# Half of the projection matmuls read their moving operand and write their PSUM bank in descending order of columns

## The chip, the cores and the metric

The kernel runs on one core of one Trainium2 chip. The metric is the device time of one execution in microseconds (us). TensorE (PE in the profile) does the matmuls, VectorE (DVE), ScalarE (ACT) and GpSimd (POOL) the elementwise work, and SyncE (SP) issues most DMAs. The time before is 3540.6 us, the median of two runs.

## The reference, cut to what matters

A sequence of 512 tokens with 1024 features goes through five blocks. Four of them have a mixer (differential attention, HGRN2, sliding-window attention, differential attention again), an output projection, a feed-forward part and a gated addition; the fifth has retention, a linear recurrence and a convolved feed-forward part. Nearly all the arithmetic is dense products of the activations with weight matrices:

```python
for i in range(DEPTH):
    ...
    h = layer_norm(ALPHA * h + y, ln_g[i, 0], ln_b[i, 0])
    u = jnp.square(jax.nn.relu(h @ w_up[i])) @ w_down[i]
    h = layer_norm(ALPHA * h + u, ln_g[i, 1], ln_b[i, 1])
    h = h + jax.nn.sigmoid(h @ w_ple_gate[i]) * (p[i] @ w_ple[i])
```

with `w_up` 1024 x 4096 and `w_down` 4096 x 1024. Each product is wanted at about float32 precision.

## The kernel before, in words

**Tiling.** Activations lie in SBUF features first: a tile such as `xh` is [128, 8, 512], that is 8 blocks of 128 features by all 512 tokens. Weights come from HBM as a stream of slabs of 1024 input features by 256 output features (1 MB each), into a ring of three or four slots. A slab used for one product is a unit of PE's work.

**Three passes.** Every operand is split into a high part and a low part of type float32r: `whi` and `wlo` of the weights, `xh` and `xl` or `gh` and `gl` of the activations. A product is the sum of three matmuls: high by high, high by low, low by high. POOL makes `whi` from `raw` (line 468), DVE makes `wlo` (line 1768).

**The loops of a unit.** A unit with features as output rows is eight calls of `feature_chunk`, one for each block k of 128 input features. A call loops over the two blocks j of 128 output features. For each it calls `passes`, whose three matmuls (lines 498, 499, 500) hold 128x128 weights in the array, stream all 512 tokens as the moving operand, and add into one whole PSUM bank, `proj[:, 2 * (u % 2) + j, :]`. So a unit fills two banks, and the next unit uses the other two of `proj`. ACT and DVE read both banks when the unit is done, always in ascending order, and release them.

**The other two forms.** `half_chunk` (lines 619 to 621) does the same for half of the tokens, 256 columns at a time, around the normalisations, where the second half of the tokens isn't ready yet. `token_chunk` (lines 531 to 533) makes values with tokens as output rows: the activations of token block `st` are the stationary operand, and 256 columns of `whi` or `wlo` the moving one; its four token blocks fill the halves of two banks.

**What stays apart.** The mixers' own matmuls (scores, transposes, values) write the `mix` banks and have their own lines: line 816 works on slices of heads in HGRN2 with a strided moving operand, line 1042 makes values of retention in plain float32. The first unit of the kernel is written out by hand in `first_chunks` (line 677), with another order: each pass goes over k and j, so that the bank changes at every matmul.

**What sets the order.** Every engine's instructions stand in a fixed order, written out by hand. PE waits at the start of a unit for the slab's split (`split_done`) and for the release of the banks used two units before (`PLAN.released`). PE's order is the program's.

Of the kernel before, what the change touches and what calls it, by code (L numbers as in the profile page):

```python
# [144 lines left out]
def cols(hf):  # L145
    return slice(0, S) if hf is None else slice(hf * HALF, (hf + 1) * HALF)
# [65 lines left out]
def build(nc, stream, xin, pin, pos, vecs, relb, onehot, eye, picks, decay, out):  # L212
    with ExitStack() as ctx:
# [203 lines left out]
        @block.sync  # L417
        def _(sp):

            for t in range(4):  # L420
                sp.dma_start(raw[0][:, 2 * t:2 * t + 2].rearrange("p k n -> p (k n)"), stream[0, :, 512 * t:512 * t + 512]).then_inc(first_in[t], 16)
            for n in range(1, N_SLABS):
                if n < 3:
                    sp.wait_ge(x_in[n + 1], 16)
                elif n == 3:
                    sp.wait_ge(raw_in[2], 16)
                else:
                    sp.wait_ge(unit_done, PLAN.last_unit[BEFORE[n]] + 1)
                if n == RETURNED:
                    sp.wait_ge(gl_ready, 4 * (G_GEN["mixed"] + 1))  # L430
                if n == 2:
                    for dst, src in (vec[:, :], vecs), (ident[:, :], eye), (tab[:, :], onehot), (rb[0:32, :], relb):
                        sp.dma_start(dst, src).then_inc(loaded, 16)
                sp.dma_start(raw[SLOT[n]][:, :, :].rearrange("p k n -> p (k n)"), stream[n]).then_inc(raw_in[SLOT[n]], 16)

            for hf in range(2):
                for t in range(KT // 2):
                    p2 = slice(2 * t, 2 * t + 2)
                    sp.wait_ge(M("final_out"), KT // 2 * hf + t + 1)
                    sp.dma_start(out[:, p2, cols(hf)], fin[:, p2, cols(hf)]).then_inc(M("stored"), 16)  # L440
            sp.wait_ge(M("stored"), KT * 16)
# [50 lines left out]

        @block.tensor
        def _(pe):
            def passes(out, wparts, xparts, first, last, check=False):

                (wh, wl), (ah, al) = wparts, xparts
                nc.tensor.matmul(out, wh, ah, start=first, stop=False, skip_group_check=check)  # L498
                nc.tensor.matmul(out, wh, al, start=False, stop=False, skip_group_check=check)  # L499
                return nc.tensor.matmul(out, wl, ah, start=False, stop=last, skip_group_check=check)  # L500
# [9 lines left out]
            def feature_chunk(u, k, kn, w0, operand):  # L510

                slot = SLOT[PLAN.unit_slab[u]]
                oh, ol = operand
                for j in range(2):
                    c = slice(j * P, (j + 1) * P)
                    last = passes(proj[:, 2 * (u % 2) + j, :], (whi[slot][:, w0 + k, c], wlo[slot][:, w0 + k, c]),
                                  (oh[:, k, :], ol[:, k, :]), k == 0, k == kn - 1)
                return last

            def token_chunk(u, k, kn, operand, c0=0, width=256, banks=(0, 1)):  # L520


                slot = SLOT[PLAN.unit_slab[u]]
                oh, ol = operand
                per = 4 // len(banks)
                for st in range(4):
                    o = proj[:, 2 * (u % 2) + banks[st // per], (st % per) * width:(st % per + 1) * width]
                    t = slice(st * P, (st + 1) * P)
                    w = slice(c0, c0 + width)
                    ah, al, wh, wl = oh[:, k, t], ol[:, k, t], whi[slot][:, k, w], wlo[slot][:, k, w]  # L530
                    nc.tensor.matmul(o, ah, wh, start=k == 0 and st % per == 0, stop=False, skip_group_check=True)  # L531
                    nc.tensor.matmul(o, ah, wl, start=False, stop=False, skip_group_check=True)  # L532
                    last = nc.tensor.matmul(o, al, wh, start=False, stop=k == kn - 1, skip_group_check=True)  # L533
                return last
# [10 lines left out]
            def whole_unit(u, which, gen=None, token=False, kn=8, w0=0, operand=None):  # L545
                begin_unit(u)
                op = operand or (X if which == "x" else G)
                for k in range(kn):
                    if gen is not None:
                        operand_wait(which, gen, k)  # L550
                    last = token_chunk(u, k, kn, op) if token else feature_chunk(u, k, kn, w0, op)
                last.then_inc(unit_done, 1)
# [10 lines left out]
            def out_chunks(layer, first, end):  # L563

                for i in range(first, end):
                    j, k = DA_TAIL[i] if layer % 3 == 0 else TAIL[i]
                    u = PLAN.at[f"out{layer}"][1] + j
                    if k == 0:
                        begin_unit(u)
                    out_operand(layer, k)  # L570
                    last = feature_chunk(u, k, 8, 0, X)
                    if k == 7:
                        last.then_inc(unit_done, 1)

            def out_halves(layer, first, end):

                for j, k in HALVES[first:end]:
                    u = PLAN.at[f"out{layer}"][1] + j
                    if k == 0:
                        pe.wait_ge(split_done, PLAN.unit_slab[u] + 1)  # L580
                    out_operand(layer, k)
                    last = half_chunk(u, k, 0, X, True, mix[:, j - 2, :])
                    if k == 7:
                        last.then_inc(M("half_done"), 1)
# [24 lines left out]
            def half_chunk(u, k, hf, operand, own_banks, bank=None):  # L609

                slot = SLOT[PLAN.unit_slab[u]]
                oh, ol = operand
                for j in range(2):
                    c = slice(j * P, (j + 1) * P)
                    o = proj[:, 2 * (u % 2) + hf, cols(j)] if own_banks else proj[:, 2 * (u % 2) + j, cols(hf)]
                    if bank is not None:
                        o = bank[:, cols(j)]
                    wh, wl, ah, al = whi[slot][:, k, c], wlo[slot][:, k, c], oh[:, k, cols(hf)], ol[:, k, cols(hf)]
                    nc.tensor.matmul(o, wh, ah, start=k == 0 and (j if own_banks else hf) == 0, stop=False, skip_group_check=True)  # L619
                    nc.tensor.matmul(o, wh, al, start=False, stop=False, skip_group_check=True)  # L620
                    last = nc.tensor.matmul(o, wl, ah, start=False, stop=k == 7, skip_group_check=True)  # L621
                return last
# [59 lines left out]
            def da_mixer(d, layer):  # L682
# [3 lines left out]
                def chunk(g, c):  # L686
                    u = u0 + 3 * g + c // 8
                    k = c % 8
                    if k == 0 and u > 1:
                        begin_unit(u)  # L690
                    if g == 0 and c < 8:
                        operand_wait("g", gen, k)
                    if layer == 0 and g == 0 and c < 16 and k % 2 == 0:
                        pe.wait_ge(*((first_lo, k // 2 + 4) if k < 6 else (split_done, 2)))
                    last = token_chunk(u, k, 8, G) if c // 8 == 2 else feature_chunk(u, k, 8, 0, G)
                    if k == 7:
                        last.then_inc(unit_done, 1)
# [82 lines left out]
            def hg_mixer(layer):  # L780
# [3 lines left out]
                def chunk(g, c):  # L784
                    u = u0 + 4 * g + c // 8
                    k = c % 8
                    if k == 0:
                        begin_unit(u)
                    if g == 0 and c < 8:
                        operand_wait("g", gen, k)  # L790
                    last = token_chunk(u, k, 8, G) if c // 8 == 2 else feature_chunk(u, k, 8, 0, G)
                    if k == 7:
                        last.then_inc(unit_done, 1)
# [285 lines left out]
            for n in range(4):  # L1079
                whole_unit(u0 + 3 * n, "g")  # L1080
                for t in range(2):
# [3 lines left out]
                    for k in range(2):  # L1085
                        last = feature_chunk(u, k, 2, 4 * (n % 2) + 2 * t, (xh[:, 2 * n:2 * n + 2, :], xl[:, 2 * n:2 * n + 2, :]))
# [1606 lines left out]
```

## Time and profile before

| | |
|---|---|
| median of 2 runs | 3540.6 us (3539.72 to 3541.49) |
| the profiled execution's own time | 3541.19 us |
| its span (first to last instruction) | 3539.4 us |
| PE | 3501.5 us busy, 99% of the span |
| DVE, ACT, POOL | 1769.1, 960.5 and 633.1 us busy (50%, 27%, 18%) |
| DMA | 332.88 MB, mean 94 GB/s |

A matmul's row in the trace has a start and a duration. Consecutive matmuls overlap in the array, so their durations add up to more than the span; what a matmul costs in a dense stream is the distance from its start to the next start. The granted clock is the share of its full speed at which TensorE was let run.

### The profile page before, as it was taken

The numbers are of one execution on the slowest core, as the hardware profiler recorded it, in microseconds if no ns is written. First come the engines' busy times: TensorE is split into PE (matmuls) and PEld (weight loads), VectorE is DVE, ScalarE is ACT, GpSimd is POOL, SyncE is SP. The second block draws the span as 40 slices with busy tenths as digits, with TensorE's granted clock in tenths as the row PEclk, the third lists the DMA queues.
The fourth block names the chain that finished last, engine by engine and source line by source line (L and its number), as shares of the span: only waits on it lengthen the run. The fifth ranks groups of instructions, "written<-read, shape, count | busy, mean of one in ns | idle before, by whom it ended". The sixth has DMA issues, their size and how long they took to land.

```text
span 3539.4 us, 44299 instructions
## 1 busy us (share of the span) xinstructions
PE 3501.5 (99%) x18416; PEld 2956.1 (84%) x18416; DVE 1769.1 (50%) x2276; ACT 960.5 (27%) x1679; POOL 633.1 (18%) x372
## 2 busy tenths in 40 slices
PE   9999999999999999999999999999999999999999
PEld 7788888889888888688888878888888888898887
DVE  5454334556653346763336455553474346563434
ACT  3562001334220013630113356210141215120102
POOL 2112111200031112031112111311121111211110
PEclk9999999999999999999999999999999999999999
DMA  5322222222122223122222221222222122322222
GB/s 206 108 74 94 95 95 94 103 85 85 65 103 98 95 84 111 60 90 95 95 97 94 101 84 72 98 96 95 84 80 99 72 95 95 107 96 95 96 95 72
DMA packets 65463, 332.88 MB, mean 94 GB/s; under 512 B 9795, under 2 KB 20291, under 8 KB 28532
## 3 DMA queue, kind: packets, MB, share of 16 engines
q1 hardware_dynamic: 44316, 303.50, 24.0%
q10 hardware_dynamic: 20952, 26.56, 2.3%
q8 instruction: 149, 2.44, 0.3%
q14 instruction: 46, 0.38, 0.0%
HBM read 326.22 MB, written 10.90 MB: 95 GB/s over the span
## 4 chain that ended last, share of the span: by engine, by line
PE 88%; DVE 6%; ACT 4%; issue 1%; POOL 1%; DMA 0%; DVEq 0%; ACTq 0%; POOLq 0%
PE proj L498 23%; PE proj L500 23%; PE proj L499 23%; PE proj L619 2%; PE proj L620 2%; PE proj L621 2%; PE proj L531 2%; PE proj L532 2%; PE proj L533 2%; DVE wlo L1768 1%; PE mix L709 1%; DVE s L1878 1%; ACT xh L1183 1%; ACT h L1186 1%; PE mix L735 1%
## 5 line engine op out<-in xcount | busy, mean ns | idle before, releaser
L468 POOL TENSOR_SCALAR whi<-raw 128x2048 fp32r<-128x2048 f32 x272 | 529.4, 1946 | 2676.3 <-DVE wlo L1768 1710.6
L498 PE MATMUL proj<-gh,whi 128*128 128x512 f32 x1952 | 775.3, 397 | 2.1 <-DVE wlo L1768 2.1
L500 PE MATMUL proj<-gh,wlo 128*128 128x512 f32 x1952 | 761.4, 390 | 0.0
L499 PE MATMUL proj<-gl,whi 128*128 128x512 f32 x1952 | 760.8, 390 | 0.0
L1768 DVE TENSOR_TENSOR wlo<-raw,whi 128x2048 fp32r<-128x2048 f32 x285 | 651.2, 2285 | 137.4 <-POOL whi L468 94.4
L498 PE MATMUL proj<-xh,whi 128*128 128x512 f32 x1760 | 692.8, 394 | 8.7 <-DVE wlo L1768 3.0
L500 PE MATMUL proj<-xh,wlo 128*128 128x512 f32 x1760 | 685.7, 390 | 0.0
L499 PE MATMUL proj<-xl,whi 128*128 128x512 f32 x1760 | 685.5, 389 | 0.0
L498 PEld LDWEIGHTS proj<-gh,whi 128*128 128x128 f32 x1952 | 367.0, 188 | 93.3 <-issue 15.6
L500 PEld LDWEIGHTS proj<-gh,wlo 128*128 128x128 f32 x1952 | 366.8, 188 | 77.5
L499 PEld LDWEIGHTS proj<-gl,whi 128*128 128x128 f32 x1952 | 367.1, 188 | 75.6 <-issue 1.9
L498 PEld LDWEIGHTS proj<-xh,whi 128*128 128x128 f32 x1760 | 330.8, 188 | 89.6 <-issue 11.5
L500 PEld LDWEIGHTS proj<-xh,wlo 128*128 128x128 f32 x1760 | 330.7, 188 | 69.6
L499 PEld LDWEIGHTS proj<-xl,whi 128*128 128x128 f32 x1760 | 331.0, 188 | 68.2 <-issue 1.4
L1487 ACT ACTIVATE rl<-proj 128x1024 f32<-128x1024 f32 x64 | 65.9, 1029 | 947.8 <-PE proj L500 929.2
L1861 DVE TENSOR_TENSOR h<-h,proj 128x1024 f32<-128x1024 f32 (+1 forms) x76 | 80.0, 1052 | 348.4 <-PE proj L500 325.3
L2302 DVE SCALAR_TENSOR_TENSOR hid<-proj,rl 128x1024 f32<-128x1024 f32 x64 | 78.4, 1224 | 317.7 <-ACT rl L1487 317.1
L619 PE MATMUL proj<-xh,whi 128*128 128x256 f32 x608 | 174.8, 288 | 3.5 <-POOL xl L463 2.2
L620 PE MATMUL proj<-xl,whi 128*128 128x256 f32 x608 | 171.9, 283 | 0.0
L621 PE MATMUL proj<-xh,wlo 128*128 128x256 f32 x608 | 171.8, 283 | 0.0
L531 PE MATMUL proj<-whi,gh 128*128 128x256 f32 x512 | 149.5, 292 | 0.0
L533 PE MATMUL proj<-whi,gl 128*128 128x256 f32 x512 | 144.8, 283 | 0.0
(321 smaller groups left out, 4333.0 us busy)
## 6 DMA issues: line engine op xcount, KB each, us to landing
raw<-in_stream SPq DMA_DIRECT2D x286, 1024.0 KB, 4.8
da_b<-bias_da ACTq DMA_DIRECT2D x16, 512.0 KB, 3.4
bias_da<-bias_rows ACTq DMA_DIRECT2D x8, 512.0 KB, 8.7
h<-in_x ACTq DMA_DIRECT2D x4, 512.0 KB, 8.7
bias_sw<-bias_table ACTq DMA_DIRECT2D x1, 2048.0 KB, 9.9
pf<-in_p ACTq DMA_DIRECT2D x4, 512.0 KB, 6.8
sw_b<-bias_sw ACTq DMA_DIRECT2D x4, 512.0 KB, 4.4
out_features<-fin SPq DMA_DIRECT2D x8, 256.0 KB, 2.4
```

The source lines that it names most:

```text
L468: nc.gpsimd.tensor_scalar(whi[SLOT[n]][:, :, :], raw[SLOT[n]][:, :, :], 1.0, 0.0, ALU.mult, ALU.add).then_inc(hi_done, 1)
L498: nc.tensor.matmul(out, wh, ah, start=first, stop=False, skip_group_check=check)
L499: nc.tensor.matmul(out, wh, al, start=False, stop=False, skip_group_check=check)
L500: return nc.tensor.matmul(out, wl, ah, start=False, stop=last, skip_group_check=check)
L531: nc.tensor.matmul(o, ah, wh, start=k == 0 and st % per == 0, stop=False, skip_group_check=True)
L533: last = nc.tensor.matmul(o, al, wh, start=False, stop=k == kn - 1, skip_group_check=True)
L619: nc.tensor.matmul(o, wh, ah, start=k == 0 and (j if own_banks else hf) == 0, stop=False, skip_group_check=True)
L620: nc.tensor.matmul(o, wh, al, start=False, stop=False, skip_group_check=True)
L621: last = nc.tensor.matmul(o, wl, ah, start=False, stop=k == 7, skip_group_check=True)
L1768: V.tensor_tensor(wlo[SLOT[n]][:, :, :], raw[SLOT[n]][:, :, :], whi[SLOT[n]][:, :, :].bitcast(F32), ALU.subtract).then_inc(*own.sig(split_ ...
L1861: ins = V.tensor_tensor(o, o, y, ALU.add)
L2302: V.scalar_tensor_tensor(hid[:, :, :], banks(u), 0.0, rl[:, :, :], ALU.max, ALU.mult).then_inc(*own.sig(rel["dve"]))
```

## The change

Three edits, all in the block of PE. In `passes`, a new argument `down` reverses the output, and both moving operands, along their columns; `feature_chunk` sets it for j = 1. In `token_chunk` the odd token blocks get their output and their moving weights reversed. In `half_chunk` j = 1 does. Since output and moving operand are both reversed, each column of the result still lands in its old place. The stationary operands, the order of the instructions, the flags that start and end an accumulation and all waits stay as they are, and `first_chunks` and the matmuls of the mixers are not touched. All three matmuls of one pass group, in all eight k, go in the same direction for a given bank (or, in `token_chunk`, half bank), so a bank is accumulated in one direction throughout.

```diff
-            def passes(out, wparts, xparts, first, last, check=False):
+            def passes(out, wparts, xparts, first, last, check=False, down=False):
                 (wh, wl), (ah, al) = wparts, xparts
+                if down:
+                    out, ah, al = out[:, ::-1], ah[:, ::-1], al[:, ::-1]
                 nc.tensor.matmul(out, wh, ah, start=first, stop=False, skip_group_check=check)
...
             def feature_chunk(u, k, kn, w0, operand):
...
-                                  (oh[:, k, :], ol[:, k, :]), k == 0, k == kn - 1)
+                                  (oh[:, k, :], ol[:, k, :]), k == 0, k == kn - 1, down=j == 1)
...
             def token_chunk(u, k, kn, operand, c0=0, width=256, banks=(0, 1)):
...
                     ah, al, wh, wl = oh[:, k, t], ol[:, k, t], whi[slot][:, k, w], wlo[slot][:, k, w]
+                    if st % 2:
+                        o, wh, wl = o[:, ::-1], wh[:, ::-1], wl[:, ::-1]
...
             def half_chunk(u, k, hf, operand, own_banks, bank=None):
...
                     wh, wl, ah, al = whi[slot][:, k, c], wlo[slot][:, k, c], oh[:, k, cols(hf)], ol[:, k, cols(hf)]
+                    if j:
+                        o, ah, al = o[:, ::-1], ah[:, ::-1], al[:, ::-1]
```

## Rows read from the trace of the kernel before

**Rows 1.** The page: span, then busy time of each engine.
```profile
span 3539.4 us, 44299 instructions
...
PE 3501.5 (99%) x18416; PEld 2956.1 (84%) x18416; DVE 1769.1 (50%) x2276; ACT 960.5 (27%) x1679; POOL 633.1 (18%) x372
```

**Rows 2.** The page: the chain that ended last, share of the span by engine.
```profile
PE 88%; DVE 6%; ACT 4%; issue 1%; POOL 1%; DMA 0%; DVEq 0%; ACTq 0%; POOLq 0%
```

**Rows 3.** Waits of PE, its longest three: us in total, times, longest.
```profile
PE mix L595 <- DVE s L1878: 5.1, 5, 2.2
PE proj L498 <- DVE wlo L1768: 5.1, 7, 1.5
PE mix L735 <- DVE post_on L2012: 3.9, 6, 0.8
```

**Rows 4.** The view of the cores: span and mean granted TensorE clock.
```profile
core 0: 3539.4 us, clock 0.998
```

**Rows 5.** A stretch: PE, PEld, DVE, ACT, POOL busy (x instructions), PEclk, DMA share, GB/s.
```profile
1200.00:1300.00 100.00, 100.00 (x442) 82.81 (x442) 39.24 (x25) 11.27 (x11) 17.28 (x9) 1.00 0.28 98
```

**Rows 6.** PE's groups by line, whole span: count, busy us, mean ns.
```profile
L498 PE MATMUL proj<-gh,whi 128*128 128x512 f32 x1952 | 775.3, 397 | 2.1 <-DVE wlo L1768 2.1
...
L498 PE MATMUL proj<-xh,whi 128*128 128x512 f32 x1760 | 692.8, 394 | 8.7 <-DVE wlo L1768 3.0 <-DVE xl L2168 2.5 <-POOL xl L463 1.5
...
L619 PE MATMUL proj<-xh,whi 128*128 128x256 f32 x608 | 174.8, 288 | 3.5 <-POOL xl L463 2.2 <-issue 1.3
...
L531 PE MATMUL proj<-whi,gh 128*128 128x256 f32 x512 | 149.5, 292 | 0.0
...
L619 PE MATMUL proj<-gh,whi 128*128 128x256 f32 x448 | 127.9, 286 | 0.0
...
L498 PE MATMUL proj<-ph,whi 128*128 128x512 f32 x64 | 25.7, 402 | 0.0
...
L619 PE MATMUL mix<-xh,whi 128*128 128x256 f32 x32 | 9.6, 302 | 0.0
```

**Rows 7.** Timeline of PE, a feed-forward unit: start us, duration us, one feature chunk.
```profile
660.26 0.39 PE L498 MATMUL proj<-xh,whi 128*128 128x512 f32 x1
660.49 0.39 PE L499 MATMUL proj<-xl,whi 128*128 128x512 f32 x1
660.72 0.39 PE L500 MATMUL proj<-xh,wlo 128*128 128x512 f32 x1
660.94 0.39 PE L498 MATMUL proj<-xh,whi 128*128 128x512 f32 x1
...
662.98 0.39 PE L498 MATMUL proj<-xh,whi 128*128 128x512 f32 x1
```

**Rows 8.** Timeline of PE, a token chunk and what follows it.
```profile
90.00 0.28 PE L533 MATMUL proj<-whi,gl 128*128 128x256 f32 x1
...
92.63 0.40 PE L498 MATMUL proj<-gh,whi 128*128 128x512 f32 x1
```

**Rows 9.** Timeline of PE in the hand-written first unit, four matmuls a row.
```profile
14.10 1.07 PE L677 MATMUL proj<-gh,whi 128*128 128x512 f32 x4
15.01 1.07 PE L677 MATMUL proj<-gl,whi 128*128 128x512 f32 x4
15.92 1.07 PE L677 MATMUL proj<-gh,wlo 128*128 128x512 f32 x4
```

**Rows 10.** Timeline of PE at line 816, moving step 2, then runs of 4.
```profile
732.76 1.07 PE L816 MATMUL mix<-hg_q,hg_m 128*128 128x128 f32 x8
733.59 0.48 PE L498 MATMUL proj<-gh,whi 128*128 128x512 f32 x1
...
742.83 1.05 PE L816 MATMUL mix<-hg_q,hg_m 128*128 128x128 f32 x8
743.64 0.48 PE L498 MATMUL proj<-gh,whi 128*128 128x512 f32 x1
```

**Rows 11.** Timeline of PE at line 1042: plain float32, two rows for each matmul.
```profile
2691.34 1.89 PE L1042 MATMUL mix<-rt_v,rt_s 128*128 128x256 f32 x8
2693.07 0.59 PE L1030 MATMUL mix<-rt_q,rt_k 128*128 128x256 f32 x2
```

## The prediction

> **What bounds the kernel now.** I read the page first: PE is busy for 3501.5 of 3539.4 us [rows 1], and the chain that ended last runs on PE for 88% of the span [rows 2]. The list of waits says the same from the other side: the longest three sources of idle time of PE are 5.1, 5.1 and 3.9 us in total [rows 3], and span less busy time leaves 38 us for all of them. The granted clock is 0.998 of full speed, which is the 2.4 GHz level [rows 4]. So the end is set by how fast matmuls follow each other, and a change to the stream of matmuls shows in full.
>
> A busy PE is not PE at its peak, so the next question is what one matmul costs. In a stretch of 100 us that holds nothing but matmuls of 512 columns there are 442 [rows 5], 0.226 us each. The timeline gives the same: twelve of them from 660.26 to 662.98, that is 2.72 / 12 = 0.227 us [rows 7]. For 256 columns, 22 follow each other from 90.00 to 92.63, or 0.120 us each [rows 8]. From the two, 256 more columns take 0.227 - 0.120 = 0.107 us, which is 2.4 columns in a ns, one a clock at the level granted. What is left of each matmul is a fixed part of 0.120 - 0.107 = 0.013 us, whatever its length. These two numbers, 0.107 us for 256 columns and 0.013 us for each matmul, are all that a reversed stream can change.
>
> **The change part by part.** Nothing is added or taken away, and no instruction changes its place on any engine; no wait is added. What changes is the step of two access patterns, from 1 to -1, in part of the matmuls.
>
> How many: the groups of line 498 hold 1952 + 1760 + 64 = 3776 matmuls [rows 6]; lines 499 and 500 have as many each, so 11328 in all, half of them with j = 1: 5664 of 512 columns. Line 619 has 608 + 448 + 32 = 1088 and line 531 has 512 [rows 6], each with two sister lines: (1088 + 512) x 3 = 4800, half of them reversed: 2400 of 256 columns. Together 8064 reversed matmuls. Each ns that a reversed matmul loses or wins is 8.1 us of the span, and 2% of the time, 71 us, is 8.8 ns for each.
>
> First cost, reading the moving operand backwards from SBUF. No row shows a descending read. The nearest are those of line 816: the moving operand has step 2 in the stretch from 732.76 to 733.59 (0.83 us for 8 rows) and runs of 4 in that from 742.83 to 743.64 (0.81 us) [rows 10]. Step 2 costs 0.02 us over 8 rows there, 2.5 ns each. They are plain float32, though, where a matmul takes several times as long: at line 1042, eight rows make four matmuls of 256 columns in 2693.07 - 2691.34 = 1.73 us, 0.43 us each [rows 11] against 0.120. So these reads had about four times the time for each column, and a read twice as slow would have hidden there. Bounds: nothing from below, and 2.5 ns x 8064 = 20 us as the price that a row shows. I take nothing, since a descending run of single steps touches the same words as an ascending one, and no more of them than a step of 2 does.
>
> Second cost, writing the bank backwards. Here no row is near: every write of the trace ascends in runs of 64 columns or more. The bound from below is nothing. The bound from above is the slowest stream that the trace has at this clock, the float32 rate [rows 11]: 0.43 - 0.12 = 0.31 us more for 256 columns and 0.62 for 512, so 5664 x 0.62 + 2400 x 0.31 = 4256 us, a time of about 7800 us. I take nothing, because the fixed part and the rate don't depend on where in PSUM the next write goes: in the hand-written first unit the bank changes at every matmul, and four matmuls take 15.92 - 15.01 = 0.91 us [rows 9], 0.2275 each, the same as where three in a row go to one bank [rows 7]. That is weak evidence: it shows that a jump between matmuls costs nothing, not that descending within one does.
>
> Third, the turn. The direction changes between the banks of a chunk and again at the next chunk: 2 turns in each of 11328 / 6 = 1888 feature chunks and 3264 / 6 = 544 half chunks, 4 in each of 1536 / 12 = 128 token chunks, 5376 in all. A turn could at best remove the fixed part: 5376 x 0.013 = 70 us. I take nothing: the rows of one chunk show the same 0.227 us from matmul to matmul whether the bank stays or changes [rows 7, 9], so the fixed part isn't the price of going back to column 0 of a bank.
>
> Fourth, what lies around. Consumers read the banks after the unit's last matmul as before. DVE, ACT and POOL are busy for at most half of the span [rows 1], their work isn't touched, and the slabs come in at the pace at which PE frees them.
>
> The sum against the profiled execution: 3539.4 + 0 us, with 1.8 us around the span in its own time of 3541.19 us, which is 0.6 us over the median. **Forecast: 3541 us.**
>
> **A rule against the change.** Every PSUM write seen ascends, and the 512-column rows run at one column a clock [rows 7]. The Trainium skill ("PSUM — Partial Sum Buffer", Specifications) states that PSUM has cachelines of 8 bytes, two float32 values, and that "any non-contiguous AP slows matmuls significantly"; "Advanced Engine Details and Errata" (PSUM Cachelines) wants every two consecutive elements contiguous. A step of -1 is adjacent but descending, and the rule doesn't say which it counts as. No row here tests it. If it counts as non-contiguous, the result is the first rival below.
>
> **The rivals.**
>
> (a) *Each reversed matmul streams at half rate.* The mechanism: at one column a clock, columns are taken two at a time, and a descending pair isn't taken as a pair, so that each column needs a turn of its own, on the reading or on the writing side. It speaks for it that 0.107 us for 256 columns leaves no slack at all, while everything strided in the trace runs at the slower float32 rate [rows 10, 11]. Against it: two neighbours in descending order still lie side by side. The price: 0.107 us for each 256 columns, 5664 x 0.214 + 2400 x 0.107 = 1212 + 257 = 1469 us, so 3541 + 1469 = 5010 us; some of PE's 38 us of waits would vanish, which gives about 5000. The side changes at 8.8 ns for each reversed matmul, some 8% of the loss for 256 columns: any real pairing fault lands far beyond.
>
> (b) *A small fixed price,* such as restarting a prefetch backwards: from 9 to 40 ns each, 3610 to 3860 us. The upper end is three times today's fixed part. Nothing in the trace speaks for it but that the fixed part exists.
>
> (c) *The turn helps,* as worked out above: 3541 - 70 = 3471 us, 2.0% faster, if each turn removes the whole fixed part. The equal distances of [rows 9] speak against it.
>
> (d) *The pattern is turned back,* so that the chip streams upwards anyhow: 3541 us, the same as the forecast.
>
> **How the numbers follow.** Forecast and (d), within 2% with a small price of up to 2.5 ns or a small gain: 0.57. (a) 0.29, with the float32 rate beyond it 0.02. (b) 0.08. (c) 0.04, half of it beyond 2%, and other gains no more. The likeliest case has a range of its own, 3525 to 3570 us: a fifth of the gain of (c) on one side, the 20 us of the step of 2 on the other. It holds 0.57 alone, so the range must take in (a): 3525 to 5015 us, which leaves out the float32 bound and most of (c). Faster by over 2%: 0.03, within 2%: 0.58, slower by over 2%: 0.39. Two per cent is about what a measurement of this kernel can tell from no change.
>
> **What would show it.** If I am right, the changed kernel has about 442 matmuls in a stretch of 100 us of a feed-forward part, and starts 0.227 us apart for both directions. If (a) is right, the timeline shows three starts 0.227 apart and then three about 0.44 apart, with some 300 matmuls in 100 us, DVE's and POOL's share falls to some 35 and 13% of a span of 5000 us, and PE's waits for DVE all but vanish. If (b), the second three are 0.24 to 0.27 apart. If (c), the first matmul after each turn starts 0.214 after the one before. The prediction fails at the second cost if descending writes are slow, and at the first if descending reads are; a kernel that reverses only one of the two would tell which.

## The result, and the profile after

The changed kernel takes 3603.95 us, the median of two runs (3602.96 to 3604.94), against 3540.6 us: a ratio of 1.0179, 95% interval 1.0135 to 1.0223. It is slower, by 63 us. That is just under the 2% that the text before used as its line; with two runs the interval reaches across that line. It is 7.9 ns for each of the 8064 reversed matmuls on average, but it isn't spread that way, as the rows show.

The page of the changed kernel, span, busy times and chain:

```profile
span 3601.2 us, 44299 instructions
...
PE 3566.6 (99%) x18416; PEld 2958.6 (82%) x18416; DVE 1763.9 (49%) x2276; ACT 959.6 (27%) x1679; POOL 630.7 (18%) x372
...
PE 88%; DVE 6%; ACT 4%; issue 1%; POOL 1%; DVEq 0%; ACTq 0%; POOLq 0%
```

The span is 61.8 us longer, PE's busy time 65.1 us, the other engines' busy times are within 5.2 us of those before [rows 1], and the chain has the same shares [rows 2]. So the loss is in PE's stream and nowhere else. Its waits and the clock say so too (waits of the changed kernel, the three that answer to [rows 3], and its view of the cores):

```profile
PE mix L599 <- DVE s L1884: 5.3, 5, 2.2
PE mix L741 <- DVE post_on L2018: 3.6, 6, 0.7
PE proj L500 <- DVE wlo L1774: 3.4, 7, 1.4
```
```profile
core 0: 3601.2 us, clock 0.999
```

The stretch of [rows 5] again, and one feature chunk of the changed kernel on the timeline, from its first matmul to that of the next. Lines 498 to 500 have become 500 to 502; the first three rows ascend, the next three descend:

```profile
1200.00:1300.00 100.00, 100.00 (x431) 80.70 (x430) 36.14 (x23) 10.41 (x10) 17.15 (x9) 1.00 0.27 95
```
```profile
670.07 0.40 PE L500 MATMUL proj<-xh,whi 128*128 128x512 f32 x1
670.31 0.39 PE L501 MATMUL proj<-xl,whi 128*128 128x512 f32 x1
670.54 0.39 PE L502 MATMUL proj<-xh,wlo 128*128 128x512 f32 x1
670.77 0.40 PE L500 MATMUL proj<-xh,whi 128*128 128x512 f32 x1
671.00 0.40 PE L501 MATMUL proj<-xl,whi 128*128 128x512 f32 x1
671.24 0.40 PE L502 MATMUL proj<-xh,wlo 128*128 128x512 f32 x1
671.47 0.40 PE L500 MATMUL proj<-xh,whi 128*128 128x512 f32 x1
```

431 matmuls in 100 us instead of 442, and 1.40 us for six instead of 1.36 [rows 7]. The reader should see that the first ascending matmul, which the change doesn't touch, is followed after 0.24 us, not 0.227. The ten ns steps of the timeline are too coarse for more, so I collected the starts in ns: in each of 887 stretches of two feature chunks (twelve matmuls in a row), the distance from start to next start, and of these the median at each place. The same for 257 stretches of half chunks. A half chunk is one call of `half_chunk`, with 256 columns. Here are all kernels of this study; "up" and "down" are the directions of the first three and the last three matmuls of a chunk:

```
distance in ns after matmul          1   2   3   4   5   6   sum | 256 columns, mean of twelve
before          (up / up)           227 227 227 227 227 227  1362 | 120.0
the change      (up / down)         238 232 227 234 239 231  1401 | 118.8
read_only       (up / down)         238 232 227 234 238 231  1400 | 118.8
write_only      (up / down)         227 227 227 227 227 227  1362 | 120.0
all_down        (down / down)       233 233 233 233 233 233  1398 | 118.3
by_k, even k    (up / up)           238 232 227 227 227 227  1378 |
by_k, odd k     (down / down)       232 240 231 233 233 233  1402 | 118.6
every_turn      (up down up / down up down) 238 231 228 234 232 231  1394 | 120.0 (not turned)
quads_down      (down / down)       233 233 233 233 233 233  1398 | 118.3
blocks32_down   (down / down)       232 231 232 231 232 231  1389 | 119.2
halves_swapped  (up / up)           227 227 227 227 227 227  1362 | 120.0
one_column_up   (up / up)           226 234 233 226 234 233  1386 | 113.7
one_column_down (down / down)       233 233 233 233 233 233  1398 | 118.0
small_down      (up / up, 256 down) 227 227 227 227 227 227  1362 | 118.3
pad256          (up / up)           227 227 227 227 227 227  1362 | 120.0
```

At 256 columns the mean hides a pattern: before, every distance is 120 ns; in the change the medians run from 115 to 122, and when all descend from 116 to 122.

A chunk of the change is 1401 - 1362 = 39 ns longer, and 1888 chunks x 0.039 = 74 us, more than the 62 us of the span. Where the difference lies shows when the distances of the two traces are subtracted matmul by matmul, since both have the same 18416 in the same order. The 9354 matmuls of 512 columns in long stretches (over 36 in a row) take 58.8 us more, 6.3 ns each. The other 1974, in short stretches between the mixers' matmuls, take 5.5 us more, only 2.8 ns each. The 4800 of 256 columns take 2.5 us less, and all the rest together is 0.2 us. So what a median from a dense stretch promises isn't met in full elsewhere.

### The profile page after: what moved, and what is told of

Same layout as the page of the kernel before. It is cut to its first block, busy times and chain, and to the rows that moved or that the text cites. A ratio compares the mean times of both kernels' runs of the same rounds, so it can differ in the third digit from the quotient of the medians.

```text
span 3601.2 us, 44299 instructions
## 1 busy us (share of the span) xinstructions
PE 3566.6 (99%) x18416; PEld 2958.6 (82%) x18416; DVE 1763.9 (49%) x2276; ACT 959.6 (27%) x1679; POOL 630.7 (18%) x372
## 4 chain that ended last, share of the span: by engine, by line
PE 88%; DVE 6%; ACT 4%; issue 1%; POOL 1%; DVEq 0%; ACTq 0%; POOLq 0%
PE proj L500 23%; PE proj L501 23%; PE proj L502 23%; PE proj L625 2%; PE proj L627 2%; PE proj L626 2%; PE proj L535 2%; PE proj L536 2%; PE proj L537 2%; DVE wlo L1774 1%; PE mix L715 1%; DVE s L1884 1%; ACT xh L1189 1%; ACT h L1192 1%; PE mix L741 1%
## 5 line engine op out<-in xcount | busy, mean ns | idle before, releaser
L500 PE MATMUL proj<-gh,whi 128*128 128x512 f32 x1952 | 791.7, 406 | 1.7 <-DVE wlo L1774 1.7
L501 PE MATMUL proj<-gl,whi 128*128 128x512 f32 x1952 | 774.7, 397 | 0.0
L500 PE MATMUL proj<-xh,whi 128*128 128x512 f32 x1760 | 707.8, 402 | 6.3 <-DVE xl L2174 2.5
L501 PE MATMUL proj<-xl,whi 128*128 128x512 f32 x1760 | 698.6, 397 | 0.0
```

## The experiments

The times in this section are medians, each with its ratio to runs of the kernel before taken on the same chip (3540.1 to 3540.9 us).

### All downwards

```diff
-  ..., k == 0, k == kn - 1, down=j == 1)
+  ..., k == 0, k == kn - 1, down=True)
-                    if st % 2:
+                    if True:
-                    if j:
+                    if True:
```

> Every matmul of the three forms, of both output blocks and all token blocks, descends, so that direction no longer changes within or between chunks (only against the mixers' own matmuls). Turn theory: the 63 us of the change are the price of 5376 turns, 11.8 ns each; with no turns left the time is 3541 us (within 10). Descending theory: each of the 8064 descending matmuls costs 7.9 ns, and with twice as many the time is 3541 + 127 = 3668 us. Start-to-start distance of 512 columns: 0.227 us by the turn theory, 0.235 by the other.

3602.37 us, ratio 1.0175 (1.0157 to 1.0193). Neither theory gives this: without turns the time doesn't come back, and with twice as many descending matmuls it doesn't double. The table shows 233 ns at every place: a steady descending stream of 512 columns costs 6 ns each, and 11328 x 0.006 = 68 us, less 4800 x 0.0017 = 8 us at 256 columns, gives 60 us against the 61 measured (subtracted matmul by matmul: 67.2 us more at 512 columns, 4.5 less at 256). In the change the same loss has another make-up: three descending matmuls cost 18 ns over 227, and the remaining 21 ns of the 39 come with the mixture of directions, partly on ascending matmuls (11 and 5 ns).

### Direction by input block

```diff
-  ..., k == 0, k == kn - 1, down=j == 1)
+  ..., k == 0, k == kn - 1, down=k % 2 == 1)
-                    if st % 2:
+                    if k % 2:
-                    if j:
+                    if k % 2:
```

> Direction goes with the block k of input features (odd k descends), not with the output block j: as many descending matmuls as in the change, but one turn in each feature or half chunk instead of two, and one instead of four in a token chunk: 2560 turns instead of 5376. Turn theory: 3541 + 2560 x 0.0118 = 3571 us. Descending theory: 3604 us, as the change. By the turn theory the slow distances stand behind the turn only, in the first three matmuls of each new direction, and the last three of the six are back at 0.227 us.

3587.25 us, ratio 1.0133 (1.0117 to 1.0149), between the two. As many descending matmuls as in the change cost less when they come six at a time. The table shows both parts: after a turn upwards 238 and 232 ns and then 227 four times, so here the ascending stream recovers after two matmuls (11 + 5 = 16 ns for the turn); the descending six take 1402 ns, four more than six steady ones. The sum for two chunks, 16 + 36 + 4 = 56 ns, x 944 pairs = 53 us, and the 256-column matmuls take 2.9 us less by the traces: 50 us, against 46 measured. On the timeline of this kernel, the third to the sixth matmul of an ascending chunk, with 0.22 and 0.23 us between the starts:

```profile
672.96 0.39 PE L502 MATMUL proj<-xh,wlo 128*128 128x512 f32 x1
673.18 0.39 PE L500 MATMUL proj<-xh,whi 128*128 128x512 f32 x1
673.41 0.39 PE L501 MATMUL proj<-xl,whi 128*128 128x512 f32 x1
673.63 0.39 PE L502 MATMUL proj<-xh,wlo 128*128 128x512 f32 x1
```

### Only the read, and only the write

```diff
-                    out, ah, al = out[:, ::-1], ah[:, ::-1], al[:, ::-1]
+                    ah, al = ah[:, ::-1], al[:, ::-1]       # read_only; write_only: out = out[:, ::-1]
```

and likewise in the token and half chunks.

> Only the moving operand is reversed where the change reverses it; the banks are written upwards, so the columns of those blocks come out in mirrored order (the values are not the reference's). If the price lies on the reading side: 3604 us and the same distances as in the change (0.238, 0.232, 0.227, 0.234, 0.239, 0.231 for the six matmuls of a feature chunk). If it lies on the writing side: 3541 us and 0.227 throughout.

> Only the output is reversed where the change reverses it; the moving operand is read upwards, so the columns of those blocks come out in mirrored order (the values are not the reference's). If the price lies on the writing side: 3604 us and the distances of the change. If it lies on the reading side: 3541 us and 0.227 us throughout. If both sides share it, each of the two runs shows a part of the 63 us.

The read alone: 3604.48 us, ratio 1.0181 (1.0165 to 1.0197), with the distances of the change to within 1 ns. The write alone: 3540.75 us, ratio 1.0000 (0.9990 to 1.0010), 227 and 120 ns throughout. The same stretch of both, read first:

```profile
1200.00:1300.00 100.00, 100.00 (x430) 80.74 (x429) 36.94 (x23) 9.64 (x11) 17.19 (x9) 1.00 0.26 91
```
```profile
1200.00:1300.00 100.00, 100.00 (x443) 82.84 (x442) 40.09 (x25) 10.48 (x10) 17.20 (x9) 1.00 0.28 102
```

So the whole loss is on the reading side, and writing a bank from its last column to its first costs nothing. The interval of the run with only the read reversed, with four runs, stays under 2%.

### Small matmuls alone

```diff
-  ..., k == 0, k == kn - 1, down=j == 1)
+  ..., k == 0, k == kn - 1, down=False)
-                    if st % 2:
+                    if True:
-                    if j:
+                    if True:
```

> All 4800 matmuls of 256 columns (half and token chunks) descend, all 11328 of 512 ascend as before. The run in which everything descended had 0.1183 us from start to start at 256 columns against 0.120 ascending, and 0.233 against 0.227 at 512. If the gain at 256 columns is a property of the descending read: 3540.9 - 4800 x 0.0017 = 3533 us, 0.2% faster, and 0.227 at 512 columns throughout. If it only came about beside descending 512-column matmuls: 3541 us.

3536.49 us, ratio 0.9988 (0.9980 to 0.9997): faster by about 4 us, half of what was expected. The distances came out as expected, 118.3 and 227 ns, and the page shows 6.3 us less of PE's busy time:

```profile
PE 3495.2 (99%) x18416; PEld 2949.3 (83%) x18416; DVE 1768.7 (50%) x2276; ACT 960.2 (27%) x1679; POOL 631.3 (18%) x372
```

The span is 4.7 us shorter (3534.7 against 3539.4), so 1.6 us went into idle time; many of these matmuls stand around the normalisations. One such wait is that for DVE's sums, 5.9 us now against 5.1 [rows 3]:

```profile
PE mix L599 <- DVE s L1884: 5.9, 5, 2.2
```

Subtracted matmul by matmul, the 4800 take 5.0 us less, not the 8 that the medians promise. The gain at 256 columns doesn't depend on descending 512-column neighbours. It is small, 0.1%, but it is a version that beats both kernels.

Something else changes at 256 columns: the record of the weight load. One of its rows before, and the same in this run:

```profile
L620 PEld LDWEIGHTS proj<-xl,whi 128*128 128x128 f32 x608 | 116.5, 192 | 0.1
L626 PEld LDWEIGHTS proj<-xl,whi 128*128 128x128 f32 x608 | 114.5, 188 | 0.1
```

The median load has 192 ns in every run whose 256-column matmuls all read upwards (in swapped halves too), and 188 or 189 in those in which they all descend, in groups or column by column, or in which the load reads one column. Beside 512 columns the load has 188 ns both in the kernel before and when all descend, and it ends 36 ns before the next matmul starts, or 41. So a longer load isn't what makes the steady 233 ns. That the gain at 256 columns comes from the shorter load would fit, but isn't shown.

### Groups of four columns, and of 32

```diff
-                if down:
-                    out, ah, al = out[:, ::-1], ah[:, ::-1], al[:, ::-1]
+                blk = lambda a: a.rearrange("p (n c) -> p n c", c=4)[:, ::-1, :]      # and c=32
+                out, ah, al = blk(out), blk(ah), blk(al)
```

in all three forms, for every matmul.

> All matmuls of the three forms take their columns in groups of four (16 bytes), the groups from last to first, each group upwards, in the read and the write. Order-within-a-group theory (the descending read loses because neighbours come in the wrong order inside a group that is fetched at once): 3541 us, 0.227 and 0.120 us. Group-order theory (it loses because the groups are fetched from last to first): as when everything descends, 3602 us, 0.233 and 0.118 us. If a jump after every four columns is costly in itself, reading or writing: over 3700 us.

> As the run with groups of four, with groups of 32 columns (128 bytes): each group upwards, the groups from last to first, 15 backward jumps in 512 columns. If the price comes from fetching ahead in larger pieces than 128 bytes, or from the overall direction: 0.233 us and 3602 us again. If pieces of up to 128 bytes are fetched as one and only steps down between neighbouring pieces of 16 bytes cost: near 0.227 us and 3545 us.

Groups of four: 3601.86 us, ratio 1.0175 (1.0161 to 1.0189), with the distances of the run in which everything descends. The order inside 16 bytes plays no part, and a backward step after every four columns costs no more than a plain descent. Groups of 32: 3593.33 us, ratio 1.0150 (1.0135 to 1.0165), 231.5 ns: still 4.5 of the 6 ns, although a descending step comes only every 32 columns. These runs reverse the groups in the write as well; that the loss is again on the reading side is taken over from the run with the write alone, not tested here.

### The halves swapped

```diff
+                blk = lambda a: a.rearrange("p (n c) -> p n c", c=a.shape[-1] // 2)[:, ::-1, :]
```

> Every matmul of the three forms takes the second half of its columns first, then the first half, each half upwards: one backward jump inside the stream. Direction theory (the price belongs to a stream that moves downwards from group to group): 3541 us, 0.227 and 0.120 us, or at most the price of one jump. Phase theory (all that counts is at which address the stream starts against the weight load): the distances change as when everything descends, 0.233 us at 512 columns.

3541.10 us, ratio 1.0002 (0.9993 to 1.0012), 227 and 120 ns. One backward jump of 512 columns' span is free, and the stream may start in its middle. It is not a price per jump either: 15 jumps cost 4.5 ns, 0.3 each, while one costs under 0.1 ns when the two traces are subtracted matmul by matmul, and 127 jumps or 511 steps cost 6 ns. Somewhere between two pieces of 256 columns and 16 of 32 the loss sets in; piece size and number of jumps change together here.

### A turn at every matmul

The edit is made in the kernel before; `feature_chunk` passes `down=j == 1`, and the 256-column forms stay upwards.

```diff
+                turned = lambda a, odd: a[:, ::-1] if odd else a
+                b = int(down)
-                nc.tensor.matmul(out, wh, ah, ...)
-                nc.tensor.matmul(out, wh, al, ...)
-                return nc.tensor.matmul(out, wl, ah, ...)
+                nc.tensor.matmul(turned(out, b), wh, turned(ah, b), ...)
+                nc.tensor.matmul(turned(out, 1 - b), wh, turned(al, 1 - b), ...)
+                return nc.tensor.matmul(turned(out, b), wl, turned(ah, b), ...)
```

> Feature chunks only: the middle one of three matmuls goes the other way, so the direction changes at each of the 11328 matmuls of 512 columns (bank and operand both reversed, values unchanged); 256-column matmuls ascend. Priced from the earlier runs: a descending matmul 6 ns, a turn to ascending 16 ns, a turn to descending 4 ns, 26 ns for each pair, 5664 x 0.026 = 147 us: 3688 us. If turns cost nothing when bank and operand are met again at the same end: 5664 x 0.006 = 34 us, 3575 us.

3594.51 us, ratio 1.0151 (1.0136 to 1.0166). My price list from the earlier runs was wrong: six turns in a chunk cost 32 ns with the three descending matmuls, less than two turns do in the change (39). Turns have no fixed price, and the table shows why adding prices fails: a disturbed matmul stands at 231 to 234 ns most of the time, whatever disturbed it, and 238 to 240 appear only at the first matmul after a turn upwards and the second after a turn downwards. Nor does every turn upwards cost 11 and 5 ns: at the third matmul of this run it leaves 228 ns and at the fifth 232, against 238 at the first. In the change and in the run by input block all turns upwards fall on the first matmul of a chunk, so those two runs can't tell the turn from its place.

### One stationary column

```diff
+                one = lambda a: a[:, 0:1].broadcast_to([P, P])
+                wh, wl = one(wh), one(wl)
```

> Everything ascends, but every stationary operand is one column read 128 times (step 0), so that the weight loads no longer sweep through SBUF; the values are not the reference's. If the sweep of the weight load is what the moving read meets (meeting theory), the distances of 512 and 256 columns change from 0.227 and 0.120 us: if its fixed part of 0.013 us is the price of meetings, to 0.216 and under 0.110, a time near 3400 us. If the weight load's place doesn't matter: 0.227, 0.120 and 3541 us.

> As the run with one stationary column, but every moving operand and output descends (values not the reference's). Meeting theory (a descending read loses because it meets the weight load's sweep differently): the same distances as the ascending run with one column. Stream theory (the descending read is slower by itself): 0.006 us more at 512 columns than the ascending run with one column, 0.002 less at 256, and some 60 us more in all.

Upwards: 3565.85 us, ratio 1.0070 (1.0055 to 1.0086). Downwards: 3599.76 us, ratio 1.0168 (1.0154 to 1.0182). Both theories miss. What the weight load reads does matter to an ascending stream: the distances become 226, 234 and 233 ns at 512 columns, and 114 instead of 120 at 256. (The values in the array change with it; that they set the time is unlikely, since the descending stream has the same values and keeps its 233 ns.) But the loads' sweep isn't the cause of the 13 ns that each matmul has beyond its columns: at 512 columns the fastest pass wins 1 ns of them, though at 256 columns 6 ns go, and the descending stream hardly notices the loads: 233 and 118 with one column as with 128. The groups of the ascending run with one stationary column show it too: a mean duration of 393 ns for the first pass, which is 394 in the kernel before [rows 6], and of 396 for the other two:

```profile
L501 PE MATMUL proj<-xl,whi 128*128 128x512 f32 x1760 | 697.0, 396 | 0.0
L502 PE MATMUL proj<-xh,wlo 128*128 128x512 f32 x1760 | 696.5, 396 | 0.0
L500 PE MATMUL proj<-xh,whi 128*128 128x512 f32 x1760 | 691.7, 393 | 8.0 <-DVE xl L2174 2.5 <-DVE wlo L1774 2.1 <-POOL xl L463 1.5
```

### The tiles moved

```diff
+        top[0] += 256
         hg_m = place("hg_m", [P, 2, S], at=top[0] + 6 * S * 4)
```

> The kernel before with the activation tiles xh, xl, gh, gl (and the small tiles behind them) moved up by 256 bytes in SBUF, so that each stream starts at another address against the weight load; order and directions as before. Address theory (0.227 us is what one relation of the two addresses gives; with one stationary column the ascending distances were 0.226, 0.234 and 0.233 us): the distances change by some ns, 3541 plus or minus 20 to 60 us. Direction theory: 0.227, 0.120 and 3541 us.

3540.12 us, ratio 1.0000 (0.9990 to 1.0009), 227 and 120 ns. Moving the activations by 256 bytes against the weights changes nothing, so a shift of that size between the two start addresses isn't what makes the 227 ns. Other shifts weren't tried.

## Why the prediction was right or wrong

**The frame held.** PE's stream sets the end; no other engine's busy time moved by more than 5.2 us, and the loss of 62 us of span is 65 us of PE's busy time. The count of 8064 reversed matmuls held. The sign for being right did not: 431 matmuls in the stretch instead of 442. The time of 3604 us lies in the range of 3525 to 5015 us, and the median is within 2%. But that is luck: the range reached past 3570 us, where the likeliest case's own ended, only to take in the half rate of (a), which didn't happen, and the median within 2% came about by a price that the forecast put at nothing. The forecast itself, 3541 us, was 63 us low: the measured time lies between the cases that I had written down, just under the lower end of (b), which began at 9 ns for each reversed matmul and 3610 us.

**The step that failed is the first cost,** reading the moving operand backwards, which I took at nothing, with 2.5 ns x 8064 = 20 us as the largest price that a row shows. With only the read reversed the whole 63 us are there, three times that bound. I had noted that the rows of the strided read are plain float32 and have about four times the time for each column [rows 10, 11]; that was the very reason why they could bound nothing here, and I should have kept the bound open rather than written 20 us. The argument that a descending run "touches the same words" was true and beside the point: groups of four columns in descending order, with ascending words inside each, cost as much as a plain descent.

**The second cost was right,** with weak evidence then: writing the bank downwards costs nothing (1.0000, 0.9990 to 1.0010), so the float32 bound of 4256 us was far off. The rule that the text weighed, of the Trainium skill ("PSUM — Partial Sum Buffer", Specifications), that any non-contiguous access pattern in PSUM slows matmuls significantly, doesn't reach a step of -1: 227 ns with it as without it. Rival (a) leaned on that rule or on a fault of pairing on the reading side; neither is there. Its half rate would have given some 300 matmuls in the stretch, and even everything descending has 430.

**The third cost had the wrong sign.** I let a turn only gain, up to 70 us. After the turn upwards at the start of a chunk the next two ascending matmuls take 16 ns more between them, and in the change 21 of the 39 ns of each chunk come with the mixture. Case (c) is out: at 512 columns no median distance of the change is under 227 ns, let alone the 214 that it needed, and at 256 columns the least is 115 where 107 was needed.

**The uniform small price of (b)** was the nearest rival in size, and its mechanism, a restart backwards with a price on every reversed matmul, is also not what happened: the price depends on the length (6 ns more at 512 columns, 1.7 ns less at 256 when all descend) and falls partly on matmuls that aren't reversed. Case (d) is out, since the direction of the read shows.

**What is shown and what stays open.** Shown: the read alone costs; order inside 16 bytes is free; one jump of half the stream is free; groups of 32 columns in descending order cost 4.5 of the 6 ns; the ascending 227 ns are lost in two of three passes when the weight load reads a single column, while the descending 233 ns don't react to that. In these runs all six distances of a chunk were 227 ns only with a stream that rises in pieces of 256 columns or more beside a weight load that sweeps its 128, and whatever broke one of the two gave 231 to 240 ns at some places. That fits two readers of SBUF, the stream and the next weight load, that get in each other's way by an amount that depends on how both move; but no run isolates this, and the two runs with one column contradict the simple form of it, in which removing the sweep would have removed the 13 ns. So the side that costs is shown, and what happens there is open. Why 256 columns gain where 512 lose isn't explained either; the 4 ns by which the weight load's record is shorter there go with the gain. The piece size between 32 and 256 columns at which the loss sets in wasn't tried, nor was a turn upwards at other places of a chunk without turns in between.

## What to carry to other kernels

In a dense stream of float32r matmuls, output order in PSUM was free and read order from SBUF was not: if a result has to come out mirrored, mirror the write, and keep the moving operand ascending when it has 512 columns. Count from start to start at each place of the pattern, not the mean duration, since the price can fall on the neighbours of what was changed. And subtract two traces matmul by matmul before multiplying a median by a count: here that product was 74 us at 512 columns, and the traces have 64. Last, a row that runs at a quarter of the rate bounds nothing for the fast one: it only shows that the cost, if there is one, was hidden there.

## What the runs showed of the hardware

- A float32r stream of 512 columns costs 227 ns from start to start ascending and 233 descending at a granted clock of 0.998; one of 256 columns 120 and 118.3, the latter the mean of distances from 116 to 122. Taken as a line through the two lengths, the descending stream has 114.7 ns for 256 more columns and 3.6 ns beside them, the ascending one 107 and 13.
- Descending PSUM writes cost nothing at either length: 227 and 120 ns, as ascending.
- After a change from descending to ascending at the start of a chunk, with three or six matmuls in each direction, the next two are 11 and 5 ns slower and the third is back at 227. With a turn at every matmul this doesn't hold: 228 and 232 ns after the other turns upwards.
- The weight load beside the stream has 188 ns; it has 192 beside 256-column matmuls that read upwards. At 512 columns it ends 36 ns before the next matmul starts, 41 when all descend.
- With a stationary operand of one column read 128 times, the ascending stream takes 226, 234 and 233 ns at the three passes and 114 at 256 columns, the descending one 233 and 118.
